# Value pages by one indirect gather for each sequence, and another order of a page's positions on chip

## What is computed

```python
    past_cmp = pool_cmp[page_table].reshape(B, past_len, NSA_KV_HEADS, 2, NSA_HEAD_DIM)
    ...
    tok = block_tokens(select_blocks(p, q_pos, total))
    tok_past = jnp.minimum(tok, past_len - 1)
    pages = page_table[bi, tok_past // PAGE_SIZE]
    kv_past = pool_slc[pages, tok_past % PAGE_SIZE, hi]
    kv_new = kv_slc[bi, jnp.clip(tok - past_len, 0, T - 1), hi]
    kv_sel = jnp.where((tok >= past_len)[..., None, None], kv_new, kv_past)
    o_slc = slc_attend(q, q_pos, tok, kv_sel, slopes)
```

## Time and profile before

| | us |
|---|---|
| median of three executions | 1134.69 (1133.3 to 1135.32) |
| profiled execution | 1134.15 |
| its span, first to last instruction | 1132.5 |
| TensorE busy | 1071.6 |
| GpSimd busy | 243.3 |
| VectorE busy | 355.7 |
| ScalarE busy | 201.2 |

### The profile page before, as it was taken

The page is one execution under the profiler, slowest core; times in us unless marked ns, Lnnn a source line. Parts: engine busy times, 40 slices in busy tenths (PEclk is TensorE's granted clock), DMA queues, the critical chain, the costliest instruction groups (busy, mean ns, idle before and its releaser), DMA issues.

```text
span 1132.5 us, 17040 instructions
## 1 busy us (share of the span) xinstructions
PE 1071.6 (95%) x6364; PEld 786.5 (69%) x6364; DVE 355.7 (31%) x849; ACT 201.2 (18%) x497; POOL 243.3 (21%) x314
## 2 busy tenths in 40 slices
PE   7899999999999999999999999895698999999996
PEld 5666666666777777777776777454676777777774
DVE  4729777532142111100023225885004211110002
ACT  3321000012231000000013223574012100001000
POOL 0706766641001011000000005266300111010000
PEclk9999999999999999999999999998798999999998
DMA  8918443330425656576343226379531533433431
GB/s 337 354 52 264 127 126 112 112 112 14 174 81 186 225 206 254 196 299 223 128 163 131 103 92 198 133 261 331 196 145 47 185 116 145 143 117 113 142 128 67
DMA packets 59407, 185.21 MB, mean 164 GB/s; under 512 B 8641, under 2 KB 39618, under 8 KB 48962
## 3 DMA queue, kind: packets, MB, share of 16 engines
q1 hardware_dynamic: 50882, 164.10, 41.5%
q0 software_dynamic: 6144, 12.59, 3.6%
q10 hardware_dynamic: 2304, 7.47, 1.8%
HBM read 180.36 MB, written 10.02 MB: 168 GB/s over the span
## 4 chain that ended last, share of the span: by engine, by line
PE 88%; issue 4%; DVE 4%; POOLq 1%; DMA 1%; POOL 1%; ACT 1%; DVEq 0%; SPq 0%
PE banks L746 30%; PE banks L512 15%; PE banks L786 15%; PE banks L718 15%; PE banks L539 2%; PE banks L687 1%; POOLq L396 1%; PE banks L585 1%; PE banks L1134 1%; PE banks L700 1%; PE banks L880 1%; PE banks L487 1%; PE banks L728 1%; DMA slabs<-in_w 1%; DVE rstd L1663 1%
## 5 line engine op out<-in xcount | busy, mean ns | idle before, releaser
L746 PE MATMUL banks<-normed,slabs 128*128 128x288 f32 x1408 | 345.1, 408 | 4.6 <-ACT normed L1243 4.6
L746 PEld LDWEIGHTS banks<-normed,slabs 128*128 128x128 f32 x1408 | 269.2, 191 | 80.1 <-issue 5.0
L786 PE MATMUL banks<-hidden,slabs 128*128 128x288 f32 x704 | 171.2, 406 | 1.5 <-issue 1.5
L718 PE MATMUL banks<-arena,phase 128*128 128x384 f32 x512 | 170.6, 490 | 0.0
L786 PEld LDWEIGHTS banks<-hidden,slabs 128*128 128x128 f32 x704 | 133.6, 190 | 39.1 <-issue 2.4
L718 PEld LDWEIGHTS banks<-arena,phase 128*128 128x128 f32 x512 | 95.6, 190 | 63.3 <-issue 0.2
L1558 POOL TENSOR_TENSOR projected<-projected,rstd 128x288 f32<-128x288 f32 x44 | 34.9, 793 | 426.5 <-ACT projected L1310 426.5
L512 PE MATMUL banks<-normed,slabs 128*128 128x288 f32 (+1 forms) x416 | 107.7, 411 | 1.2 <-ACT normed L1243 1.2
L512 PEld LDWEIGHTS banks<-normed,slabs 128*128 128x128 f32 (+1 forms) x416 | 75.5, 187 | 26.2 <-ACT normed L1243 3.2
L1655 DVE TENSOR_TENSOR normed<-normed 128x288 f32<-128x288 f32 x24 | 11.0, 459 | 199.0 <-ACT normed L1303 199.0
L1310 ACT ACTIVATE projected<-projected 128x288 f32<-128x288 f32 x44 | 19.5, 442 | 281.1 <-DVE projected L1702 281.1
(11 more groups left out here) (302 smaller groups left out, 1064.8 us busy)
## 6 DMA issues: line engine op xcount, KB each, us to landing
slabs<-in_wfi SPq DMA_DIRECT2D x44, 1024.0 KB, 4.9
slabs<-in_w SPq DMA_DIRECT2D x24, 1024.0 KB, 5.0
arena<-in_cmp SPq DMA_DIRECT2D x128, 192.0 KB, 2.8
slabs<-in_wfo SPq DMA_DIRECT2D x32, 704.0 KB, 4.0
arena<-in_slck POOLq DMA_DIRECT2D x64, 96.0 KB, 3.1
arena<-in_slck SPq DMA_DIRECT2D x64, 96.0 KB, 3.4
out_win_old<-in_winold SPq DMA_DIRECT2D x8, 762.0 KB, 6.4
arena<-in_slcv SPq DMA_DIRECT2D x48, 96.0 KB, 4.1
```

Of the source, the lines that this page charges most:

```text
L718: ins = nc.tensor.matmul(out.rearrange("p h (g s) -> p h g s", s=8), W1S[:, c, a, j, :], PG[b % 2][:, :, c * 8 + j, :, :].rearrange("p g h ...
L746: return nc.tensor.matmul(BK[2 * (u % SLOTS) + c][:, 0:T], wt[:, k, c * P:c * P + P], Hn[:, k, :], start=(k == 0), stop=(k == KC - 1), ski ...
L786: ins = nc.tensor.matmul(BK[b][:, 0:T], wt[:, k, :], HD[:, 11 * kh + k, :], start=(kh + k == 0), stop=(kh * 11 + k == 21))
```

## The change

A sequence's values now come by one indirect DMA. The value cache is seen as rows of 16 positions (12,288 bytes, 8 rows a page). Partition p of sequence b takes row 8 x page_table[b, p // 8] + p % 8; a new input of 128 x 9 integers has the page numbers repeated eight times and p % 8, and GpSimd works the rows out once, in float32, with three small operations. The number loads for values, and the value loads of SyncE and ScalarE, are gone: all eight gathers stand on GpSimd.

With that, partition p holds 16 neighbouring positions of one page, so the 128 positions that one product takes are no longer one page but every sixteenth position. Scores are put in that order: the pages' keys are stored with the position in another order, the key product reads its moving data in runs of 8 elements, the scores are written in 16 runs of 32, the distances are made in the new order, and the mask becomes 128 columns for each head (32 blocks, each four times), kept in "projected".

```diff
+        PR_I, PR_F, ROWS = sb("page_rows", B + 1, I32), sb("page_rows_f", B + 1), sb("value_rows", B, U32)
...
-        MS = MISC[:, 279:378].rearrange("p (h j) -> p h j", h=H)
+        MS = Z_[:, 15 * T:15 * T + H * P].rearrange("p (h n) -> p h n", h=H)
...
-        def load_value_pages(eng, b, numbers, first=0, at_=None):
-            for n, r in enumerate(numbers):
-                a = 192 * (first + n)
-                eng.dma_start(VAL[b][:, a:a + 192], page(slcv_in, r)).then_inc(vpage_loaded[b if at_ is None else at_], 16)
+        def load_values(pool, b):
+
+            wait_value_slot(pool, b)
+            nc.gpsimd.indirect_dma_start(VAL[b], None, slcv_in, bass.IndirectOffsetOnAxis(ap=ROWS[:, b:b + 1], axis=0),
+                                         bounds_check=slcv_in.shape[0] - 1).then_inc(vpage_loaded[b], 16)
...
-                    ins = nc.tensor.matmul(BK[7][32 * b:32 * b + 32, :].rearrange("p (g n) -> p g n", n=P), QBD[:, b, h, :],
-                                           KP[c % 2][:, b, :, h, :], start=True, stop=True)
+                    ins = nc.tensor.matmul(BK[7][32 * b:32 * b + 32, :].rearrange("p (j g a) -> p j g a", g=4, a=8),
+                                           QBD[:, b, h, :], KP[c % 2][:, b, :, h, :].rearrange("p g (j a) -> p j g a", a=8),
+                                           start=True, stop=True)
...
-                    pe.wait_ge(vpage_loaded[b], 16 * NPG)
+                    pe.wait_ge(vpage_loaded[b], 16)
...
-            values = value_numbers(ACTE, 7, 0, 12)
-            wait_value_slot(act, 7)
-            load_value_pages(act, 7, values)
...
+            pool.wait_ge(rows_loaded, 16)
+            ch.step(nc.gpsimd.tensor_copy(PR_F[:, :], PR_I[:, :]))
+            ch.step(nc.gpsimd.tensor_scalar(PR_F[:, 0:B], PR_F[:, 0:B], 8.0, PR_F[:, B:B + 1], ALU.mult, ALU.add))
+            ch.step(nc.gpsimd.tensor_copy(ROWS[:, :], PR_F[:, 0:B]))
...
-            values.append(value_numbers(POOL, 1))
-            wait_value_slot(pool, 0)
-            load_value_pages(pool, 0, values[0])
...
+            for b in (0, 6, 3, 1, 2, 4, 5, 7):
+                load_values(pool, b)
...
-                ch.step(ts(MS, IMP, 0.5 * TAKEN, NEG, ALU.is_gt, ALU.mult))
+
+                for h in range(H):
+                    src = IMP[:, h, 0:NBLK].unsqueeze(2).to_broadcast([P, NBLK, 4])
+                    ch.tick(ts(MS[:, h, :].rearrange("p (k i) -> p k i", i=4), src, 0.5 * TAKEN, NEG, ALU.is_gt, ALU.mult))
+                ch.sync()
...
-                banks.give(stt(S_SLC[:, h, WIN * c:WIN * c + WIN], SLCD[:, WIN * c:WIN * c + WIN], slope[:, h:h + 1],
-                               BK[7][:, :], ALU.mult, ALU.add), ("sk", c, h))
+                rows = lambda x: x.rearrange("p (j n) -> p j n", j=16)
+                banks.give(stt(rows(S_SLC[:, h, 0:PAST])[:, :, 32 * c:32 * c + 32], rows(SLCD[:, WIN * c:WIN * c + WIN]),
+                               slope[:, h:h + 1], rows(BK[7][:, :]), ALU.mult, ALU.add), ("sk", c, h))
...
-                blk = S_SLC[:, h, 0:PAST].rearrange("p (j i) -> p j i", i=64)
-                mask = MS[:, h, 0:NBLK].unsqueeze(2).to_broadcast([P, NBLK, 64])
+                blk = S_SLC[:, h, 0:PAST].rearrange("p (j n) -> p j n", n=P)
+                mask = MS[:, h, :].unsqueeze(1).to_broadcast([P, 16, P])
...
+            sp.dma_start(PR_I[:, :], rows_in).then_inc(rows_loaded, 16)
...
-            values = {2: value_numbers(SP, 2)}
...
-            values[5] = value_numbers(SP, 5)
-            for b in (2, 4, 5):
-                wait_value_slot(sp, b)
-                load_value_pages(sp, b, values[b])
-            values[7] = value_numbers(SP, 7, 12)
-            load_value_pages(sp, 7, values[7], first=12)
...
-    slcd = (np.arange(PAST)[None, :] - PAST - t).astype(f)
+    slcd = (np.arange(PAST).reshape(4, 4, 8, 16).transpose(0, 3, 1, 2).reshape(1, PAST) - PAST - t).astype(f)
...
-    slck = slc[:, :, :, 0].transpose(0, 3, 2, 1).reshape(pool, 64, H * PAGE)
-    slcv = slc[:, :, :, 1].reshape(pool, PAGE, H * 64)
+    slck = slc[:, :, :, 0].reshape(pool, 8, 16, H, 64).transpose(0, 4, 3, 2, 1).reshape(pool, 64, H * PAGE)
+    slcv = slc[:, :, :, 1].reshape(pool * 8, 16 * H * 64)
+    table = a["page_table"].astype(np.int32)
+    rows = np.concatenate([np.repeat(table.T, 8, axis=0), np.arange(P, dtype=np.int32)[:, None] % 8], 1)
```

More of the change, by code:

```diff
@@ L14 @@
 I32 = mybir.dt.int32
+U32 = mybir.dt.uint32
 ALU = mybir.AluOpType
@@ L17 @@
 AX_X = mybir.AxisListType.X
-SP, POOL, ACTE = mybir.EngineType.SP, mybir.EngineType.Pool, mybir.EngineType.Activation
+SP, POOL = mybir.EngineType.SP, mybir.EngineType.Pool
 P = 128
@@ L340, in trunk_kernel @@
         memkv_stored, state_stored = sem("mem_kv_stored"), sem("state_stored")
[L341 removed]
+        stored, pt_loaded, rows_loaded = sem("stored"), sem("page_table_loaded"), sem("page_rows_loaded")
         hid_done = sem("last_hidden_done")
@@ L391, in key_numbers @@
             return numbers
-        def value_numbers(which, b, first=0, end=NPG):
-            numbers = []
-            for p0 in range(NPG * b + first, NPG * b + end, 4):
-                numbers += nc.values_load_multi_w_load_instructions(PT[0:1, p0:p0 + 4], engines=[which], min_val=0,
-                                                                    max_val=slcv_in.shape[0] - 1)[1]
-            return numbers
         def load_key_pages(eng, c, parity, numbers):
@@ L2394 @@
                   wglu=slabs(a["ssm_w_glu"][0]), wfi=wfi, wfo=wfo, w1s=w1s, w1p=w1p,
-                  pages=a["page_table"].reshape(1, P).astype(np.int32), cmp=cmp_pages, slck=slck, slcv=slcv, wink=wink,
+                  pages=table.reshape(1, P), rows=rows, cmp=cmp_pages, slck=slck, slcv=slcv, wink=wink,
                   winv=winv, memk=memk, memv=memv, winold=win[:, TS:].reshape(B, WIN - TS, H * 128))
```

13 lines of the change are left out of this document (1 added, 12 removed).

## The result

The changed kernel takes 1127.05 us (median of 4, 1126.35 to 1128.61) against 1135.01 us (median of 4, 1133.3 to 1136.13) before: a ratio of 0.9932, with a 95% interval of 0.9917 to 0.9947. That is 8.0 us less, where 11.5 was forecast, and 1127.05 instead of 1122.7 us (the sum started from 1134.15). The direction and the range held; terms of the sum were mis-sized, and the question of this study is which.

What follows compares the result with a forecast made beforehand. TensorE holds 95% of the span, so only its waits, 18.6 us before the value products, could be won. Gathers were to end the second half at 806.2 instead of 817.7: 1134.15 - 11.5 = 1122.7 us, range 1118 to 1132.

Steps and rivals of the forecast that it cites:

- pace: Value gathers on the DMA engines: 12 KB rows move at 430 GB/s, 3.66 us a gather; the other end is 4.64.
- issue: GpSimd's issue of a gather: 0.55 us taken, as for one page of 128 descriptors; upper end 9.38 or 10.2 us.
- cover: Row numbers, mask, runs of 32 in scores and of 8 in key products: hidden or at full rate, so zero.
- rival A: Value gathers come at the old 339 GB/s: gain only 2.6 to 5.7 us, 1128.4 to 1131.5 us; chance 0.15.
- rival B: GpSimd cannot issue the seven gathers after 768.9 fast enough: 9.38 us each, 27.4 us slower, 1161.6 us; chance 0.13.
- rival C: Runs of 8 slow the key products (line 1087): at double cost 12.8 us more, about 1135.5 us; chance 0.04.
- The head of the line: GpSimd's queue: sequences 1 and 2, free at 763.0, stand behind 6 until 768.9, a cost of nearly 6 us.
- the 1.2 us for the slab beside the last gather: Before the second half: the first output slab meets the last gather's tail, moving its landing from 797.0 to 798.2.
- The fixed part: Start of the string of gathers after 768.9: 2.5 us once, taken from a page's landing of 2.7 us.
- a first half that starts after 790: Sign of a wrong forecast, at the value products' first half, which was forecast to start at 786.0.
- The length of the halves: Value products (line 1134): 8.6 us for the first half, 8.05 for the second, as in the earlier trace.
- The best end of the prediction: No slab beside the last gather, second half at the upper clock in 6.0 us: 14.7 us less, 1119.4 us.

Runs made afterwards that it cites:

- x10_order_third: Second repeat of the changed kernel with its gathers issued in the order 0, 1, 2, 3, 6, 4, 5, 7: 1120.84 us.
- x1_order: Changed kernel with gathers issued in the order 0, 1, 2, 3, 6, 4, 5, 7 instead of 0, 6, 3, 1, 2, 4, 5, 7: 1120.57 us.
- x9_quiet: Changed kernel without the gathers of sequences 4, 5 and 7, and with the first output slab loaded after the second half: 1124.44 us, one run.
- x2_slab_late: Changed kernel with the first output slab loaded after the second half of the value products, not after the first: 1128.91 us.
- x4_direct: Changed kernel with gathers undone, each page one transfer of 8 rows of 12 KB on its former queue, new position order kept: 1174.49 us.
- x3_three_less: Changed kernel without the gathers of sequences 4, 5 and 7, whose products read the pages of 1, 2 and 3: 1120.44 us, one run.
- x6_half_rows: Changed kernel in the order 0, 1, 2, 3, 6, 4, 5, 7, each sequence by two gathers of 6 KB rows: 1125.39 us.

## Why the prediction was right and where it was wrong

**Direction, pace, issue, cover: right.** The string of gathers moved at 430 GB/s as taken from the earlier trace rows, not at the 339 of rival A. In its queue a gather begins some 3.7 us after the one before it (x10_order_third: first packets at 781.94, 785.69 and 789.37). An issue costs 1.0 to 2.7 us, under the 3.66 us up to which it is free; rival B fell. The Trainium skill's GPSIMD Engine Reference, section Performance pitfalls for Q7 kernels, gave an estimated 10.9 us by its price for each index; the rows of 1.0 to 2.7 us do not show it. The key products last as long as before (605 ns at the median in both), so rival C fell as well, and VectorE's score writes in runs of 32 cost nothing (746 ns at the median, 748 in the earlier trace rows). TensorE's key products before and after, and VectorE's score writes after, minimum/median/maximum in ns:

```profile
L1087 PE MATMUL banks<-arena,phase x96: 592/605/697, 715.6 to 762.4; 128*32 128x512 f32 x96
```

```profile
L1083 PE MATMUL banks<-arena,phase x96: 592/605/957, 716.1 to 763.1; 128*32 128x512 f32 x96
```

```profile
L2051 DVE SCALAR_TENSOR_TENSOR phase<-phase,phase_small,banks x12: 737/746/748, 719.3 to 763.7; 128x512 f32<-128x512 f32 x12
```

The head of the line was named too: "nearly 6 us in which the DMA engines could have worked". x1_order and its two repeats put its price on the chip: 5.0 to 6.5 us below 1127.05, or 5.0 to 5.4 by the ratios to before (0.9888, 0.9887 and 0.9884 against 0.9932). Not found was the 1.2 us for the slab beside the last gather: the slab was asked for at 800.38, and that gather landed at 800.80, 3.67 us after the one before it, like the others.

**The fixed part: mis-sized, 2.5 us taken, 5.6 found.** Product 1117 ends at 768.77 + 0.83 = 769.6. Four gathers at 3.66 us make 784.2; sequence 2 landed at 789.86. Of the 5.6 us, 0.9 pass until GpSimd issues (770.50), 1.8 until the first packet moves (772.34), and the first gather takes 4.9 us after the idle stretch (its last row packet ends at 777.22) instead of 3.66; the rest, some 1.6 us, is the tail. As many rows as four gathers have had ended by 788.30, 1.6 us before sequence 2 landed, while the very last row of the string ended 0.4 us before its landing; so it seems that the engines do not finish together, and the landing is told after the last of them. The row of a page, 546 ns and 2.7 us, was the nearest to be had, but a page's landing is a median of transfers that follow each other, not of one that starts on idle engines. Together with the 0.7 us by which product 1117 stands later in this profile, the first half began at 790.10 instead of 786.0. That is the first error, 4.1 us, and it meets one of the prediction's own signs of being wrong, "a first half that starts after 790".

**The length of the halves: the step that failed.** The prediction took 8.6 and 8.05 us from the earlier trace rows, and let the first output slab touch only the landing of the last gather (1.2 us). Measured were 10.7 (790.10 to 800.80) and 11.95 us. The transfers that the gathers bring closer together do not slow the products themselves (x10_order_third: 243 in 5.44 us beside 425 GB/s, 22.4 ns each; x1_order: 128 in 2.84 us, 22.2 ns each, at 19 GB/s and less); they delay the products' instructions. Nothing in the sum had a place for that: the pages before left refills only 0.6 to 1.4 us late, and no row shows one. x9_quiet gives what the halves need with nothing beside them, 15.75 us, under the 16.65 of the prediction; in the changed kernel they took 22.8. The best end of the prediction, 6.0 us for a half at the upper clock, left the refills out as well: the second half of x9_quiet, at a granted clock of 1.00, took 7.1.

**The sum of the errors.** Start of the first half +4.1, its length +2.1, the wait before the second half -3.5 (3.6 forecast, 0.13 found, since the longer first half hid the last landings), its length +3.9: together 6.6, and the second half ends at 812.88, 6.7 us later than the forecast 806.2. Against that, 3.1 us came back behind it as clock, which the sum had not counted. 11.5 - 6.7 + 3.1 = 7.9. So the near miss is partly luck: a larger error in the halves was softened by the projection, and by 1.4 us in line 742 that three profiles of one kernel show as scatter.

**The clock.** In the prediction the first half kept 8.6 us because "a wait remains". That held: after a wait the granted clock is 0.50, the lower level, for the first 4 us in before, here (790.1) and in x9_quiet. In x10_order_third, where TensorE waits only 0.94 us ahead, it is 1.00 from 784.0 to 789.5 and 243 products take 5.4 us instead of 7.5; then TensorE outruns its refill and pauses for 3.08 us. Windows of that run:

```profile
784.00:789.50 5.50, 5.44 (x243) 5.16 (x244) 0.00 (x0) 1.14 (x2) 0.00 (x0) 1.00 1.01 425
789.50:792.60 3.10, 0.03 (x4) 0.03 (x4) 0.00 (x0) 0.00 (x0) 0.00 (x0) 1.00 0.99 414
```

**What stays open.** In which order a DMA engine serves the packet of instructions among what is queued, and when TensorE asks for it, was not settled: the delay did not shrink when the rows were halved (4.1 us in the first half against 3.6) or when the slab came in quarters (3.2 us after TensorE went on, against 2.4 to 2.6 in the three profiles of the order alone). That the packet's start and TensorE's stop fall within 0.02 us of each other in the changed kernel is not explained either; in x2_slab_late and x10_order_third the packet begins 1.0 us (798.11 and 799.11) before the stop, or after it (790.28 and 789.50). How much of the gain is the single issue and how much the longer rows no run parts, since x4_direct changed both. x3_three_less and x9_quiet are single runs, read by their traces.

The best version measured is the gather in the order 0, 1, 2, 3, 6, 4, 5, 7: 1120.57, 1122.00 and 1120.84 us in three comparisons, ratios to before of 0.9888, 0.9887 and 0.9884 (the last 0.9862 to 0.9906).

## What to carry to other kernels

Where a queue hands out transfers in order, sort it by the time at which the places come free and by who is waited for first; a wait at its head can idle all DMA engines, and here that cost some 5 to 6.5 us where the whole change brought 8. Where TensorE runs many short products, its instructions are themselves DMA traffic: look for pauses that the profile calls issue, 256 instructions apart, before pressing bulk loads against such a stretch, and count what later loads give back. A string of transfers that starts on idle engines should be costed with a start of its own, here 5.6 us, not with the landing of one in mid-stream.

## What the runs showed of the hardware

- TensorE's instructions came in packets of 16 KB, one for 256 instructions. Beside quiet engines the next packet began 0.5 to 1.1 us after a block was entered (x3_three_less, x9_quiet, x1_order), beside gathers 2.5 to 4.1 us, and TensorE paused for up to 3.4 us (x6_half_rows, first half) where the block ran out first. Behind a wait of TensorE it began 0.99 us after TensorE went on, 2.4 to 4.0 us beside a slab. The Trainium skill's page Runtime: NRT & Kernel Launch, section Instruction fetch mechanics, describes this refill in blocks of 256 instructions and calls its cost mostly hidden; here it was not.
- The same skill's page DMA: Bandwidth & Descriptors, section Queues, rings and completion order, lets a DMA engine change between queues after a packet of some 9 to 17 descriptors. A gather gives each engine 8 rows of 0.46 us, an estimated 3.7 us, near the 2.5 to 3.6 us found in the first half; with half rows it would be half, and x6_half_rows showed 4.1. So the rule does not account for it.
- An indirect gather of 128 rows cost GpSimd 1.0 to 2.7 us whether a row had 6 or 12 KB, the longer ones (1.6 us and more) between 767 and 781 us. A busy VectorE does not tell them apart: it is busy for 2.93 of 3.00 us from 777 on, and for 3.93 of 4.00 us from 763 to 767 in x10_order_third, where two issues took 1.0 and 1.1 us.
- Transfers to 8 partitions in rows of 12 KB ran at 173 GB/s in all, with the DMA engines half busy, against 430 for gathers of 128 rows.
